# A transformer layer on one core: another hand-written order in the opening, in attention's normalisation and at the end of the output projection

## The chip, the cores and the metric

The kernel runs on one core of a Trainium2 chip as one program. The metric is the device time of one execution in microseconds. TensorE (PE in the rows) multiplies; ScalarE (ACT), VectorE (DVE) and GpSimd (POOL) work on rows of 128 partitions; SyncE (SP) issues most transfers. Each engine runs its own instruction list in order, and waits on semaphores that other engines count up.

## The reference, cut to what matters

The layer is computed for two groups of tokens, 512 of a prompt and 1024 of a sample, 1024 channels each, in fp32:

```
mod = silu(c) @ w_ada + b_ada           # shift1, scale1, gate1, shift2, scale2, gate2
h   = rmsnorm(x, g_attn) * (1 + scale1) + shift1
u, q, k, v = split(h @ w_in, 4)         # 512 columns each
q, k = rmsnorm(q, g_q), rmsnorm(k, g_k) # per head of 64
f = fourier_mix(u, w_fmix)              # real part of a 2-D DFT, then a map per group of 128
a = softmax(q k' / 8 + bias) v          # in a window of 8 rows x 16 columns of the token grid
mix = concat(rmsnorm(f), rmsnorm(a)) @ w_o
x = x + gate1 * mix
h2 = rmsnorm(x, g_ffn) * (1 + scale2) + shift2
x = x + gate2 * ((silu(h2 @ w_gate) * (h2 @ w_up)) @ w_down)
```

## The kernel before

Every fp32 product is made of three matmuls of a rounded upper half and the remaining lower half of each operand: `mm3`, lines 101 to 103. So each operand is first split: a copy that rounds (`h_hi`, `win_hi`, `wo_hi`, `wff_hi`) and a subtraction (`h_lo` and so on). The 1536 tokens are three chunks of 512 (c = 0 to 2), and 12 tiles of 128 (t). Channels are eight pieces of 128 (k). One K-step is one `mm3` on 512 tokens.

There is no planner. Each stage has a function for each engine (`run_pe`, `run_act`, ...), and the order of the calls in it is the order of the instructions on that engine.

**Opening** (`opening`). SyncE loads the first third of w_ada in eight pieces of 1 MB, x in three parts of 2 MB, and the first columns of w_in (line 282). TensorE makes the first modulation rows from the eight pieces (L674), and turns x chunk by chunk: `turn_x(n)`, n = 8c + k, four 128x128 transposes (L668) into one of two PSUM banks that change with n (`x_bank`). ScalarE modulates the turned x (`modulate`, L443). VectorE rounds it (L545) and makes the lower half for even k (L548); GpSimd makes the lower half for odd k (L349). Then TensorE runs, for each chunk, eight K-steps for u columns s = 0 and eight for s = 1. After c = 0 it turns k = 0 and 1 of c = 1. The other two thirds of w_ada come in 16 pieces through a ring of five buffers, and `rest_products` multiplies them, two at a time (`pieces_at`), between these passes. The row norms of x need squares: of each chunk's four tiles ScalarE makes two (L430) and VectorE two (L526), then ScalarE the root and VectorE the reciprocal and the scaled rows (L535). Six tiles of u columns follow (`tile(1, i)`). ScalarE evacuates each u tile (`stage_u`, L449) and GpSimd stores it to DRAM (`store`, L353).

**Attention** (`attention`): 48 steps, one for each pair of heads, column block and chunk. In step s TensorE turns the probabilities of pair s - 1 (L995), turns v tokens in two of three steps (L972), makes the scores of pair s + 1 (L986), spreads the softmax's reciprocal of pair s - 1 over 64 partitions for each head by a matmul of a broadcast column with the identity (`spread`, L1004), and multiplies probabilities by v (L1020). ScalarE makes two exponentials (L867), copies half of the turned probabilities (L875), in one of three steps v tokens (L889), and the spread scale (L881). VectorE makes the reciprocal, adds bias and takes maxima (L914), and scales the output. In the second 24 steps VectorE also does one `fold` of u each for the Fourier stage.

**Second half** (`second_half`). 48 mixing tiles: `mix_out(m)` is four K-steps of w_o columns n = m // 12 on token tile t = m % 12. VectorE gates each (L1664), GpSimd adds it to x (L1729). Row norm, turns (L1794), modulation (L1565) and split (L1681, L1684 on VectorE, L1735 on GpSimd for odd k of c = 0) give h2. Norm 0 comes before the last four mixing tiles, two turns of c = 0 after each of these, and the turns of c = 1 and c = 2 stand between the K-steps of the first gate tile on the chunk before. The feed-forward part then loops over 11 pairs of weight tiles; `pair(0)` is the first.

Other stages (q, k, v projections from 152.8 to about 360 us, Fourier from 497 to 547) lie between these.

Of the kernel before, what the change touches and what calls it, by code (L numbers as in the profile page):

```python
# [18 lines left out]
ALU = mybir.AluOpType  # L19
# [86 lines left out]
def layer(nc, x_prompt, x_sample, w_ada, b_ada, vec_rows, w_in, w_fmix, rpb_pad, masks, dft_c, dft_t1,  # L106
          dft_t0, w_o, w_gate, w_up, w_down, u_scratch, gate_rows, y_prompt, y_sample):
    ctx = ExitStack()
    with ctx:
# [42 lines left out]
        kept.u_in, kept.wf_in, kept.cs_in = [sem(f"u_in{r}") for r in range(2)], sem("wf_in"), sem("cs_in")  # L152
# [47 lines left out]
def opening(nc, at, sem, banks, kept):  # L200
# [54 lines left out]

    def x_bank(n):

        return ((2, 5), (2, 5), (0, 3))[n // KT][n % 2]
# [8 lines left out]
    def pieces_at(n):  # L267

        return {3: (0, 1), 4: (2, 3), 5: (4, 5), 6: (6, 7), 7: (8, 9), 8: (10, 11), 9: (12, 13), 10: (14, 15)}.get(n, ())

    with nc.Block() as block:
        @block.sync
        def _(sp):
# [11 lines left out]
            def load_ada(q):  # L285
                half, k = divmod(q, KT)
                if q >= 5:
                    sp.wait_ge(ada_used, q - 4)
                sp.dma_start(ada[q % 5][:], w_ada[128 * k:128 * k + 128, 4 * CH * (half + 1):4 * CH * (half + 2)]
                             ).then_inc(ada_in[q % 5], 16)  # L290
# [26 lines left out]
            load_ada(0)  # L317
            load_ada(1)
            sp.wait_ge(x_turned, 2 * KT)
            load_ada(2)  # L320
            load_ada(3)
            sp.wait_ge(x_turned, 3 * KT)
            load_ada(4)
            load_ada(5)
            load_ada(6)
# [3 lines left out]
            for q in range(7, PIECES):  # L329
                load_ada(q)  # L330
# [13 lines left out]
        def _(pool):  # L344
# [5 lines left out]

            def store(j, i, s, c):
                pool.wait_ge(bank_free, 6 * j + i + 1)
                pool.dma_start(u_scratch[(2 * j + s) * 128:(2 * j + s) * 128 + 128, CH * c:CH * c + CH],  # L353
                               u_stage[:, i % 2]).then_inc(u_stored[i % 2], 16)
# [20 lines left out]
            for c in range(NCH):  # L375
                for k in range(1, KT, 2):
                    split(KT * c + k)
                for s in range(2):
                    store(0, 2 * c + s, s, c)
            for i in range(6):  # L380
                store(1, i, *divmod(i, NCH))
                if i == 2:
                    store_gate(0)
            store_gate(1)
            rounds(pool, 0, J_QK - J_U, sq_lows)
            for s in range(2):
                pool.wait_ge(u_stored[s], 16 * 3 * J_U)
# [35 lines left out]
        def _(act):  # L423
# [22 lines left out]
            def stage_u(j, i, bank):  # L446
                act.wait_ge(z_summed, 6 * j + i + 1)
                after(act, u_stored[i % 2], 16 * (3 * j + i // 2))
                act.activation(u_stage[:, i % 2], banks[:, bank], ACT.Copy).then_inc(bank_free, 1)  # L449
# [33 lines left out]
            split_hi(act, 0, 1)  # L483
# [3 lines left out]
            square(4)  # L487
            square(5)
            root(1)
            stage_u(0, 0, 0)  # L490
            for k in range(KT):
                modulate(KT + k)
                if k in (0, 3):
                    square(8 + k // 3)
                if k == 1:
                    stage_u(0, 1, 3)
                if k == 5:
                    root(2)
            stage_u(0, 2, 1)
            for k in range(KT):  # L500
                modulate(2 * KT + k)
                if k == 3:
                    stage_u(0, 3, 4)
            split_hi(act, 1, 0)
            split_hi(act, 1, 1)
            stage_u(0, 4, 2)
            stage_u(0, 5, 5)
            for i in range(6):
                stage_u(1, i, i)
# [9 lines left out]
        def _(dve):  # L519
# [76 lines left out]
            split_lo(dve, 0, 0)  # L596
# [8 lines left out]
            split_lo(dve, 0, 1)  # L605
            for k in range(KT):
                split(k)
            square(6)
            square(7)
# [12 lines left out]
            for i in range(6):  # L622
                if i == 1:
                    rest_rows(0)
                if i == 2:
                    rest_mod(0)
                if i == 5:
# [1311 lines left out]
```

## Time and profile before

| | |
|---|---|
| runs | 1792.05, 1794.22, 1794.43 us; median 1794.22 |
| the profiled execution | 1798.47 us, its span 1796.5 us |
| TensorE busy over the span | 1741.6 us, 97% |
| VectorE, GpSimd, ScalarE busy | 804.7, 524.7, 431.3 us |
| first 44 mixing tiles and sums, 547.09 to 675.56 | TensorE busy 128.47 of 128.47 us |
| feed-forward from the third tile on, 747.30 to the end | TensorE busy 1044.70 of 1049.20 us |
| mean granted TensorE clock over the span | 0.990 |

All durations come from the one profiled execution; its own time is 4.25 us above the median of the runs. Matmuls overlap, so the spacing of starts, and not the length of one, tells what a matmul costs. A wait in square brackets behind a row is the idle time ahead of that instruction, and names what ended it. The time base is the start of the span.

### The profile page before, as it was taken

To read this page: it belongs to the slowest core of one execution; us is meant where nothing else is said; L and a number is where in the kernel's file an instruction comes from. 1 tells how busy PE (TensorE), PEld (TensorE's weight loads), DVE (VectorE), ACT (ScalarE), POOL (GpSimd) and SP (SyncE) were. 2 spreads that over 40 slices of the span, in tenths; PEclk is the share of its full clock that TensorE was granted. 3 is DMA by queue.
4 is the path that set the end of the run, shared out by engine and by line. 5 is a ranking of instruction groups with operands and counts; after the bars stand their busy time and mean duration, and the time that the engine had idled before them with its cause. 6 is when DMAs were issued, how large, how long until landed. Compare 5 with 4: busy or idle time off the path is not lost.

```text
span 1796.5 us, 22022 instructions
## 1 busy us (share of the span) xinstructions
PE 1741.6 (97%) x8437; PEld 1387.4 (77%) x8437; DVE 804.7 (45%) x1244; ACT 431.3 (24%) x779; POOL 524.7 (29%) x435
## 2 busy tenths in 40 slices
PE   5799999999999997999999999999999999999998
PEld 2557888866768885788888888888888888888887
DVE  3513886057874427352433425261524334242525
ACT  3312332177762016211111110101021111101110
POOL 0311221077736442040221405050503123050505
PEclk9999999999999998999999999999999999999999
DMA  9381014063113101001011110111010101110113
GB/s 352 141 324 39 25 34 77 12 139 78 49 36 133 55 1 47 24 24 47 24 35 35 35 35 23 35 35 35 12 47 23 47 23 35 35 35 23 35 35 140
DMA packets 98543, 108.70 MB, mean 61 GB/s; under 512 B 19655, under 2 KB 82337, under 8 KB 95161
## 3 DMA queue, kind: packets, MB, share of 16 engines
q1 hardware_dynamic: 97401, 104.82, 18.5%
q0 software_dynamic: 1088, 3.16, 0.5%
q8 instruction: 34, 0.56, 0.1%
q14 instruction: 20, 0.16, 0.0%
HBM read 98.51 MB, written 9.45 MB: 60 GB/s over the span
## 4 chain that ended last, share of the span: by engine, by line
PE 77%; DVE 2%; issue 0%; ACT 0%; POOL 0%; DVEq 0%; ACTq 0%; POOLq 0%
PE banks L101 22%; PE banks L102 22%; PE banks L103 22%; PE banks L986 2%; PE banks L995 2%; PE banks L1325 2%; PE banks L1020 2%; PE banks L1004 1%; PE banks L972 1%; DVE h_hi L1681 0%; PE banks L1794 0%; DVE xn L1674 0%; DVE h_lo L1684 0%; PE banks L1308 0%; ACT t_second L1565 0%
## 5 line engine op out<-in xcount | busy, mean ns | idle before, releaser
L1748 POOL TENSOR_TENSOR x<-x,ff_scratch 128x512 f32<-128x512 f32 x198 | 263.1, 1361 | 834.7 <-DVE ff_scratch L1641 834.1
L101 PE MATMUL banks<-h_hi,wff_hi 128*128 128x512 f32 x1056 | 414.1, 392 | 10.9 <-POOL h_lo L1735 6.1
L102 PE MATMUL banks<-h_lo,wff_hi 128*128 128x512 f32 x1056 | 412.1, 390 | 0.0
L103 PE MATMUL banks<-h_hi,wff_lo 128*128 128x512 f32 x1056 | 411.9, 390 | 0.0
L1500 DVE TENSOR_TENSOR wff_lo<-wff_raw,wff_hi 128x1024 fp32r<-128x1024 f32 x66 | 81.5, 1236 | 405.3 <-ACT wff_hi L1496 405.2
L101 PEld LDWEIGHTS banks<-h_hi,wff_hi 128*128 128x128 f32 x1056 | 199.2, 189 | 52.0 <-issue 9.3
L103 PEld LDWEIGHTS banks<-h_hi,wff_lo 128*128 128x128 f32 x1056 | 199.0, 188 | 41.5
L102 PEld LDWEIGHTS banks<-h_lo,wff_hi 128*128 128x128 f32 x1056 | 199.2, 189 | 40.3
L1641 DVE TENSOR_TENSOR ff_scratch<-banks,gate 128x512 f32<-128x512 f32 x264 | 177.3, 687 | 72.0 <-PE banks L103 49.3
L103 PE MATMUL banks<-wff_hi,ff_lo 128*128 128x512 f32 x528 | 205.4, 389 | 0.0
L102 PE MATMUL banks<-wff_lo,ff_hi 128*128 128x512 f32 x528 | 205.4, 389 | 0.0
L101 PE MATMUL banks<-wff_hi,ff_hi 128*128 128x512 f32 x528 | 205.4, 389 | 0.0
L1496 ACT ACTIVATE wff_hi<-wff_raw 128x1024 fp32r<-128x1024 f32 x66 | 70.0, 1060 | 437.5 <-DMA wff_raw<-in_w_up 354.1
L101 PE MATMUL banks<-h_hi,win_hi 128*128 128x512 f32 x384 | 153.8, 401 | 14.4 <-POOL h_lo L349 12.3
L103 PE MATMUL banks<-h_hi,win_lo 128*128 128x512 f32 x384 | 150.8, 393 | 0.0
L102 PE MATMUL banks<-h_lo,win_hi 128*128 128x512 f32 x384 | 150.6, 392 | 0.0
L101 PEld LDWEIGHTS banks<-wff_hi,ff_hi 128*128 128x128 f32 x528 | 99.2, 188 | 20.6
L103 PEld LDWEIGHTS banks<-wff_hi,ff_lo 128*128 128x128 f32 x528 | 99.1, 188 | 20.5
L102 PEld LDWEIGHTS banks<-wff_lo,ff_hi 128*128 128x128 f32 x528 | 99.1, 188 | 20.5
L1628 DVE TENSOR_TENSOR ff_raw<-banks,ff_scratch 128x512 f32<-128x512 f32 x66 | 45.5, 689 | 138.0 <-PE banks L103 138.0
L101 PEld LDWEIGHTS banks<-h_hi,win_hi 128*128 128x128 f32 x384 | 72.5, 189 | 38.9 <-POOL h_lo L349 15.1
L1526 ACT ACTIVATE ff_hi<-ff_raw 128x512 fp32r<-128x512 f32 x66 | 41.7, 632 | 243.5 <-DVE ff_raw L1628 243.5
(169 smaller groups left out, 2106.0 us busy)
## 6 DMA issues: line engine op xcount, KB each, us to landing
ada_rest<-in_w_ada SPq DMA_DIRECT2D x16, 1024.0 KB, 8.6
wff_raw<-in_w_gate SPq DMA_DIRECT2D x22, 512.0 KB, 4.7
wff_raw<-in_w_up SPq DMA_DIRECT2D x22, 512.0 KB, 3.9
wff_raw<-in_w_down SPq DMA_DIRECT2D x22, 512.0 KB, 3.2
ada<-in_w_ada SPq DMA_DIRECT2D x8, 1024.0 KB, 13.8
win_raw<-in_w_in SPq DMA_DIRECT2D x16, 512.0 KB, 3.9
x_first<-in_x_sample SPq DMA_DIRECT2D x2, 2048.0 KB, 16.5
wo_raw<-in_w_o SPq DMA_DIRECT2D x4, 1024.0 KB, 5.0
```

The costliest lines, as they stand in the source:

```text
L101: pe.matmul(out, lhs[0], rhs[0], start=start, stop=False)
L102: pe.matmul(out, lhs[0], rhs[1], start=False, stop=False)
L103: return pe.matmul(out, lhs[1], rhs[0], start=False, stop=stop)
L986: pe.matmul(banks[:, hh, 0:n], queries, keys, start=True, stop=True).then_inc(qk_done, 1)
L995: last = pe.transpose(banks[:, 2 + hh, 128 * j:128 * j + 128], s_ring[:, w % 2, hh, 128 * j:128 * j + 128], ident[:])
L1020: last = pe.matmul(banks[64 * hh:64 * hh + 64, 4 + w % 2, 0:128], v_tok[:, b * NVT + V_TILE0[c] + j, 64 * hh:64 * hh + 64], pt_ring[:, w % ...
L1496: act.activation(w_hi[:, i % 3], w_raw[:, i % 3], ACT.Copy).then_inc(w_split_hi, 1)
L1500: dve.tensor_tensor(w_lo[:, i % 3], w_raw[:, i % 3], w_hi[:, i % 3].bitcast(F32), ALU.subtract).then_inc(w_ready, 1)
L1526: act.activation(ff_hi[:, f, CH * c:CH * c + CH], ff_raw[:, f, CH * c:CH * c + CH], ACT.Copy).then_inc(ff_hi_s, 1)
L1628: dve.tensor_tensor(part, banks[:, 3 + c], scratch[:, c], ALU.mult).then_inc(product, 1)
L1641: dve.tensor_tensor(scratch[:, n % 3], banks[:, (6 + n) % 8], gate2[:, REQ[t // 4], 512 * half:512 * half + 512], ALU.mult).then_inc(d_gat ...
L1748: pool.tensor_tensor(part, part, scratch[:, n % 3], ALU.add).then_inc(d_added, 1)
```

## The change

In the opening all eight pieces of the first w_ada load stand ahead of w_in in SyncE's queue, and two of the later pieces are loaded without a wait. `x_bank` uses three banks, so that `turn_x(n)` waits for the modulation of n - 3 and not n - 2. Five turns of c = 1 stand in the second pass of c = 0, the other three in the first pass of c = 1, and all eight of c = 2 in the second pass of c = 1. The later pieces of w_ada come one place earlier, and the modulation turn stands before the six tiles. Squares of c = 1 stand among the modulations (ScalarE) and splits (VectorE) of c = 0. ScalarE issues the stores of u.

In attention ScalarE first copies the two reciprocals of a pair of heads to 64 columns each (`widen`, a 128x128 array), and TensorE transposes that array at the head of the next step. The output scaling comes one step later. The folds start at step 12 and take 36 steps.

In the second half the mixing tiles of n = 2 and 3 go chunk by chunk (`SEQ`). The turns of c = 0 stand behind mixing tiles 34 to 37, those of c = 1 behind 42 to 45, and those of c = 2 within the second and third first-pair tiles. The row norm is two rows on VectorE and two on ScalarE instead of three and one, and all odd lower halves are GpSimd's.

```diff
@@ opening
+    SLOT = (0, 1, 0, 1, 2, 3, 0, 1, 2, 3, 4, 0, 1, 2, 3, 4)
...
-        return ((2, 5), (2, 5), (0, 3))[n // KT][n % 2]
+        return ((2, 5, 7), (2, 5, 7), (0, 3, 7))[n // KT][n % KT % 3]
...
-        return {3: (0, 1), 4: (2, 3), 5: (4, 5), 6: (6, 7), 7: (8, 9), 8: (10, 11), 9: (12, 13), 10: (14, 15)}.get(n, ())
+        return (2 * n - 2, 2 * n - 1) if 1 <= n <= 8 else ()
...
-            for k in range(3, 6):
+            for k in range(3, KT):
                 load_ada0(k)
             load(0, 0)
-            load_ada0(6)
-            load_ada0(7)
             load(0, 1)
             load_x(1)
             load_x(2)
+            load_ada(0)
+            load_ada(1)
...
+                act.wait_ge(bank_free, 6 * j + i + 1)
+                act.dma_start(u_scratch[(2 * j + s) * 128:(2 * j + s) * 128 + 128, CH * c:CH * c + CH],
+                              u_stage[:, i % 2]).then_inc(u_stored[i % 2], 16)
...
             for k in range(KT):
                 split(k)
-            square(6)
-            square(7)
+                if k in (3, 5):
+                    square(6 + k // 5)
+                if k == 4:
+                    split_lo(dve, 0, 1)
...
-                if n >= 2:
-                    pe.wait_ge(t_ready, n - 1)
+                if n >= 3:
+                    pe.wait_ge(t_ready, n - 2)
...
-                    if c == 1 and k == 3:
-                        turn_x(2 * KT)
-                        turn_x(2 * KT + 1)
+                    if c == 0 and k >= 3:
+                        turn_x(KT + k - 3)
+                    if c == 1:
+                        turn_x(2 * KT + k)
@@ attention
+    FOLD_STEPS = list(range(PAIRS_A // 4, PAIRS_A // 2)) + list(range(PAIRS_A // 2, PAIRS_A, 2))
...
+        def widen(w):
+            act.wait_ge(recip_done, w + 1)
+            if w >= 2:
+                act.wait_ge(scale_spread, w - 1)
+            act.activation(recips[:, w % 2].rearrange("p (h f) -> p h f", h=2),
+                           bass.AP(stats, 4 * PAIRS_A + 2 * w, [[6 * PAIRS_A, 128], [1, 2], [0, HEAD]]), ACT.Copy
+                           ).then_inc(widened, 1)
...
-            if s:
-                copy_scale(s - 1)
+            if s >= 2:
+                copy_scale(s - 2)
+            if 1 <= s <= PAIRS_A:
+                widen(s - 1)
...
-            for hh in range(2):
-                last = pe.matmul(banks[64 * hh:64 * hh + 64, 6, 0:128],
-                                 stats[:, 2, 2 * w + hh:2 * w + hh + 1].broadcast_to((128, 64)), ident[:],
-                                 start=True, stop=True)
-            last.then_inc(scale_spread, 1)
+            pe.transpose(banks[:, 6, 0:128], recips[:, w % 2], ident[:]).then_inc(scale_spread, 1)
@@ second_half
+    SEQ = [(n, t) for n in range(2) for t in range(TT)] + [
+        (n, t) for c in range(NCH) for n in range(2, OS) for t in range(4 * c, 4 * c + 4)]
+    FIRST = [SEQ.index((n, 0)) for n in range(OS)]
+    TURN = [34, 42]
...
+        square(8)
+        square(9)
+        square(10)
+        split_hi(act, 0, 1)
+        square(11)
+        root(2)
+        norm(2)
+        silu(act, 0, 0)
...
+            ff_tile(0, 0)
+            h_ready(1)
+            pe.wait_ge(gated, TT * OS - 2)
+            for k in range(KT):
+                ff_step(0, 1, k)
+                if k >= 2:
+                    turn(2 * KT + k - 2)
+            pe.wait_ge(w_ready, 2)
...
+            mix_out(m)
+            for c, first in enumerate(TURN):
+                if first <= m < first + 4:
+                    turn(KT * c + 2 * (m - first))
+                    turn(KT * c + 2 * (m - first) + 1)
```

The first place is TensorE's list in the opening where c = 0's second pass ends and c = 1's first begins, of before (`x_first` is x, `ident` the identity of a transpose):

```order
L101 MATMUL banks<-h_hi,win_hi 128x512
L102 MATMUL banks<-h_lo,win_hi 128x512
L103 MATMUL banks<-h_hi,win_lo 128x512
L668 MATMUL banks<-ident,x_first 128x128 x12
L101 MATMUL banks<-h_hi,win_hi 128x512
L102 MATMUL banks<-h_lo,win_hi 128x512
L103 MATMUL banks<-h_hi,win_lo 128x512
L668 MATMUL banks<-ident,x_first 128x128 x4
L101 MATMUL banks<-h_hi,win_hi 128x512
L102 MATMUL banks<-h_lo,win_hi 128x512
L103 MATMUL banks<-h_hi,win_lo 128x512
```

and of the kernel after, where L659 is the same transpose and L665 the product of the later w_ada pieces:

```order
L659 MATMUL banks<-ident,x_first 128x128 x4
L101 MATMUL banks<-h_hi,win_hi 128x512
L102 MATMUL banks<-h_lo,win_hi 128x512
L103 MATMUL banks<-h_hi,win_lo 128x512
L659 MATMUL banks<-ident,x_first 128x128 x4
L665 MATMUL banks<-ada_rest_73,silu_c 2x512 x4
L665 MATMUL banks<-ada_rest_74,silu_c 2x512 x4
L101 MATMUL banks<-h_hi,win_hi 128x512
L102 MATMUL banks<-h_lo,win_hi 128x512
L103 MATMUL banks<-h_hi,win_lo 128x512
L659 MATMUL banks<-ident,x_first 128x128 x4
L101 MATMUL banks<-h_hi,win_hi 128x512
```

The twelve transposes that stood in one block between the passes (with the next four behind the first K-step) have moved, four at a time, between the K-steps of the second pass; a pair of w_ada pieces stands in the gap.

The second place is TensorE's list in three steps of attention, of before (`s_ring` holds probabilities, `v_pair` values, `stats` the reciprocals):

```order
L1004 MATMUL banks<-ident,stats 64x128 x2
L1020 MATMUL banks<-pt_ring,v_tok 64x128 x6
L995 MATMUL banks<-ident,s_ring 128x128 x4
L972 MATMUL banks<-ident,v_pair 128x128 x4
L986 MATMUL banks<-z 128x384 x2
L1004 MATMUL banks<-ident,stats 64x128 x2
L1020 MATMUL banks<-pt_ring,v_tok 64x128 x4
L995 MATMUL banks<-ident,s_ring 128x128 x6
L972 MATMUL banks<-ident,v_pair 128x128 x2
L986 MATMUL banks<-z 128x256 x2
L1004 MATMUL banks<-ident,stats 64x128 x2
L1020 MATMUL banks<-pt_ring,v_tok 64x128 x6
```

and of after (L1006 is the new transpose, of `recips`):

```order
L1006 MATMUL banks<-ident,recips 128x128
L998 MATMUL banks<-ident,s_ring 128x128 x4
L975 MATMUL banks<-ident,v_pair 128x128 x4
L989 MATMUL banks<-z 128x384 x2
L1019 MATMUL banks<-pt_ring,v_tok 64x128 x4
L1006 MATMUL banks<-ident,recips 128x128
L998 MATMUL banks<-ident,s_ring 128x128 x6
L975 MATMUL banks<-ident,v_pair 128x128 x2
L989 MATMUL banks<-z 128x256 x2
L1019 MATMUL banks<-pt_ring,v_tok 64x128 x6
L1006 MATMUL banks<-ident,recips 128x128
```

Two matmuls between the scores and the values of a step have become one at the step's head, ahead of the turn of the probabilities. On ScalarE the same three steps stood so before:

```order
L867 ACTIVATE s_ring,stats<-s_ring,stats 128x384
L875 ACTIVATE pt_ring<-banks 128x256
L867 ACTIVATE s_ring,stats<-s_ring,stats 128x384
L889 ACTIVATE v_tok<-banks 128x512
L881 ACTIVATE scale_sb<-banks 128x128
L867 ACTIVATE s_ring,stats<-s_ring,stats 128x384
L875 ACTIVATE pt_ring<-banks 128x384
L867 ACTIVATE s_ring,stats<-s_ring,stats 128x384
L881 ACTIVATE scale_sb<-banks 128x128
```

and stand so after (L874 copies the spread scale, L881 widens the reciprocals):

```order
L860 ACTIVATE s_ring,stats<-s_ring,stats 128x384
L868 ACTIVATE pt_ring<-banks 128x256
L860 ACTIVATE s_ring,stats<-s_ring,stats 128x384
L890 ACTIVATE v_tok<-banks 128x512
L874 ACTIVATE scale_sb<-banks 128x128
L881 ACTIVATE recips<-stats 128x128
L860 ACTIVATE s_ring,stats<-s_ring,stats 128x384
L868 ACTIVATE pt_ring<-banks 128x384
L860 ACTIVATE s_ring,stats<-s_ring,stats 128x384
L874 ACTIVATE scale_sb<-banks 128x128
L881 ACTIVATE recips<-stats 128x128
```

In each step the widening has come in behind the copy of the scale, and in the step with `v_tok` both stand behind that copy.

The third place is TensorE's list in the mixing, where the first turns of c = 0 stand; of before, behind mixing tile 44:

```order
L102 MATMUL banks<-wo_lo_2399,h_hi 128x512
L103 MATMUL banks<-wo_hi_2398,h_lo 128x512
L1794 MATMUL banks<-ident,xn 128x128 x8
L101 MATMUL banks<-wo_hi_2398,h_hi 128x512
L102 MATMUL banks<-wo_lo_2399,h_hi 128x512
```

and of after, behind mixing tile 34 (L1790 is the turn, `xn_early` the two halves of the normed rows):

```order
L102 MATMUL banks<-wo_lo_2363,h_hi 128x512
L103 MATMUL banks<-wo_hi_2362,h_lo 128x512
L1790 MATMUL banks<-ident,xn_early_2404 128x128 x2
L1790 MATMUL banks<-ident,xn_early_2405 128x128 x2
L1790 MATMUL banks<-ident,xn_early_2404 128x128 x2
L1790 MATMUL banks<-ident,xn_early_2405 128x128 x2
L101 MATMUL banks<-wo_hi_2362,h_hi 128x512
L102 MATMUL banks<-wo_lo_2363,h_hi 128x512
L103 MATMUL banks<-wo_hi_2362,h_lo 128x512
```

The turns have moved ten tiles up, in front of other mixing tiles, and read the rows from two arrays.

## Rows read from the trace of the kernel before

**Rows 1.** Busy time by stretch (start:end, length, engines, clock, DMA): opening, attention, mixing's end.

```profile
36.65:152.83 116.18, 101.34 (x512) 68.17 (x513) 42.28 (x64) 32.54 (x49) 26.79 (x25) 0.96 0.54 206
361.00:497.00 136.00, 134.50 (x1265) 93.04 (x1264) 99.73 (x378) 100.46 (x307) 101.50 (x112) 0.97 0.40 88
...
675.56:747.30 71.74, 58.30 (x277) 47.35 (x277) 43.69 (x67) 35.38 (x50) 11.31 (x8) 0.90 0.11 37
```

**Rows 2.** TensorE's timeline in the opening: start, length, line, idle before and its releaser.

```profile
38.13 0.47 PE L101 MATMUL banks<-h_hi,win_hi 128*128 128x512 f32 x1 [0.82 <-DVE h_lo L548]
...
49.66 0.50 PE L101 MATMUL banks<-h_hi,win_hi 128*128 128x512 f32 x1 [1.63 <-POOL h_lo L349]
...
50.46 0.40 PE L101 MATMUL banks<-h_hi,win_hi 128*128 128x512 f32 x1
...
51.83 0.39 PE L101 MATMUL banks<-h_hi,win_hi 128*128 128x512 f32 x1
...
78.99 1.90 PE L674 MATMUL banks<-ada_rest,silu_c 128*2 128x512 f32 x16
80.82 0.66 PE L668 MATMUL banks<-ident,x_first 128*128 128x128 f32 x4
```

**Rows 3.** TensorE's timeline, the two last pieces of the first w_ada load.

```profile
28.34 1.89 PE L674 MATMUL banks<-ada,silu_c 128*2 128x512 f32 x8 [2.33 <-DMA ada<-in_w_ada]
30.93 1.89 PE L674 MATMUL banks<-ada,silu_c 128*2 128x512 f32 x8 [0.70 <-DMA ada<-in_w_ada]
```

**Rows 4.** GpSimd's (POOL) and then VectorE's (DVE) timeline beside each other in the opening.

```profile
44.72 1.28 POOL L349 TENSOR_TENSOR h_lo<-t_first,h_hi 128x512 fp32r<-128x512 f32 x1 [1.89 <-DVE h_hi L545]
47.42 2.18 POOL L349 TENSOR_TENSOR h_lo<-t_first,h_hi 128x512 fp32r<-128x512 f32 x1 [1.43 <-DVE h_hi L545]
...
47.26 1.22 DVE L526 CUSTOM_DVE_ANT_0 dump_dve<-x_first 128x1024 f32<-128x1024 f32 x1
...
48.63 2.05 DVE L526 CUSTOM_DVE_ANT_0 dump_dve<-x_first 128x1024 f32<-128x1024 f32 x1
```

**Rows 5.** Attention: TensorE's timeline of one step and a head, then ScalarE's (ACT).

```profile
374.68 0.44 PE L1004 MATMUL banks<-ident,stats 128*64 128x128 f32 x4
374.95 0.83 PE L1020 MATMUL banks<-pt_ring,v_tok 128*64 128x128 f32 x12
375.71 0.66 PE L995 MATMUL banks<-ident,s_ring 128*128 128x128 f32 x4
376.20 0.60 PE L972 MATMUL banks<-ident,v_pair 128*128 128x128 f32 x4
...
378.38 0.88 PE L995 MATMUL banks<-ident,s_ring 128*128 128x128 f32 x6
...
375.17 0.28 ACT L881 ACTIVATE scale_sb<-banks 128x128 f32<-128x128 f32 x1 [0.58 <-PE banks L1004]
...
377.06 0.58 ACT L889 ACTIVATE v_tok<-banks 128x512 f32<-128x512 f32 x1
```

**Rows 6.** TensorE's timeline, the first feed-forward K-step after the last mixing tile.

```profile
695.15 0.77 PE L101 MATMUL banks<-h_hi,wff_hi 128*128 128x512 f32 x1 [6.11 <-POOL h_lo L1735]
```

**Rows 7.** SyncE's issues: a backlogged pair, then all of line 289, shortest/median/longest.

```profile
5.71 15.02 SPq L275 DMA_DIRECT2D ada<-in_w_ada  x2
...
L289 SPq DMA_DIRECT2D ada_rest<-in_w_ada x16: 327/430/1207, 46.8 to 130.6; - x16
...
DMA to landing us min/median/max: 4.9/8.6/13.5
```

**Rows 8.** The page's costliest groups, and its DMA issues with their time to landing.

```profile
L1500 DVE TENSOR_TENSOR wff_lo<-wff_raw,wff_hi 128x1024 fp32r<-128x1024 f32 x66 | 81.5, 1236 | 405.3 <-ACT wff_hi L1496 405.2
...
L1496 ACT ACTIVATE wff_hi<-wff_raw 128x1024 fp32r<-128x1024 f32 x66 | 70.0, 1060 | 437.5 <-DMA wff_raw<-in_w_up 354.1
...
wff_raw<-in_w_up SPq DMA_DIRECT2D x22, 512.0 KB, 3.9
...
wo_raw<-in_w_o SPq DMA_DIRECT2D x4, 1024.0 KB, 5.0
```

More of the change, by code:

```diff
@@ L1026, in run_pe @@
         turn_v(0, 1)
-        for s in range(PAIRS_A + 1):
-            if s:
+        for s in range(PAIRS_A + 2):
+            if s >= 2:
+                spread(s - 2)
+            if 1 <= s <= PAIRS_A:
                 turn(s - 1)
@@ L1699, in run_dve @@
                 mix_recip(1)
-            if m % TT == 1 and m > TT and m // TT + 1 < OS:
-                split_o(m // TT + 1)
-        norm(0)
-        for i in range(4):
-            gate_mix(TT * OS - 4 + i)
-            if i == 2:
-                split_lo(dve, 0, 0)
-            split(2 * i)
-            split(2 * i + 1)
-        norm(1)
-        for k in range(KT):
-            split(KT + k)
+            if m in (FIRST[1] + 1, FIRST[2] + 1):
+                split_o(2 + (m > FIRST[2]))
+            if m == FIRST[3]:
+                split_lo(dve, 0, 0)
+            for c, first in enumerate(TURN):
+                if m == first - 1:
+                    norm(c)
+                if first <= m < first + 4:
+                    split(KT * c + 2 * (m - first))
+                    split(KT * c + 2 * (m - first) + 1)
         norm(2)
@@ L1821, in run_pe, with ff_tile, h_ready, first_tiles @@
-        waits_split(pe, KT * NCH - 1)
+                last.then_inc((g_summed, u_summed)[kind], 1)
+        def ff_tile(i, c):
+            for k in range(KT):
+                ff_step(i, c, k)
+        def h_ready(c):
+            waits_split(pe, KT * c + KT - 2)
+            waits_split(pe, KT * c + KT - 1)
+        def first_tiles():
+            pe.wait_ge(w_ready, 1)
+            h_ready(0)
+            pe.wait_ge(gated, TT * OS - 3)
+            ff_tile(0, 0)
+            h_ready(1)
+            pe.wait_ge(gated, TT * OS - 2)
+            for k in range(KT):
+                ff_step(0, 1, k)
+                if k >= 2:
+                    turn(2 * KT + k - 2)
+            pe.wait_ge(w_ready, 2)
+            pe.wait_ge(gated, TT * OS)
+            for k in range(KT):
+                ff_step(1, 0, k)
+                if k < 2:
+                    turn(3 * KT - 2 + k)
+            h_ready(2)
+            ff_tile(0, 2)
+            pe.wait_ge(t_ready, NCH * KT)
+            ff_tile(1, 1)
+            ff_tile(1, 2)
@@ L1860, in pair @@
                 last.then_inc(d_summed, 1)
+        for m in range(TT * OS):
+            if m == 2 * TT - 6:
+                f_sums()
+            mix_out(m)
+            for c, first in enumerate(TURN):
+                if first <= m < first + 4:
+                    turn(KT * c + 2 * (m - first))
+                    turn(KT * c + 2 * (m - first) + 1)
         pair(0)
```

290 lines of the change are left out of this document (121 added, 169 removed).

## The prediction

> **What bounds the kernel now.** I read the share of busy time by stage first, then TensorE's own timeline in the stages that the change touches. In [rows 1] TensorE is busy 134.50 of 136.00 us in attention, and the stage table ahead shows the same of the feed-forward loop and of the first 44 output-projection tiles: work alone sets these. Two stretches differ. The opening up to 152.83 has 101.34 busy of 116.18, and the stretch from the last mixing tiles to the third feed-forward tile pair has 58.30 of 71.74, at a granted clock of 0.90. Nothing outside TensorE is full anywhere: ScalarE, the nearest, is at 100.46 of 136.00 in attention. So a microsecond is won where TensorE waits or runs below full clock, or where one of its matmuls goes.
>
> **Opening.** A K-step is three matmuls. At full clock [rows 2] show one starting at 50.46 and the second after it at 51.83: 0.685 each, 0.228 a matmul. A pair of pieces of the rest of w_ada takes 80.82 - 78.99 = 1.83, a turn of four transposes about 0.40. From the first K-step at 38.13 to 152.83 are 114.7 us. In them stand 48 K-steps of u (32.7), 21 turns (8.4), 8 pairs (14.6), 6 tiles of 8 K-steps (32.8) and some 1.4 of modulation rows: 89.9. The other 24.8 are lost to waits and to half clock. [Rows 2] show one place, 1.63 before 49.66 on GpSimd's lower half of h, and c=1 has more of them; between c=0 and c=1 turn, modulation and split run one after the other with TensorE waiting for each.
>
> The change alters each. (a) All eight pieces of the first w_ada load come ahead of w_in. In [rows 3] the piece behind w_in is waited for 2.33, the next one 0.70; the difference, 1.6 to 1.7, goes, and the first K-step comes at 36.4. The lower half of the first w_in part stays one VectorE instruction ahead of the splits, so it costs nothing new. (b) With three banks and five turns of c=1 inside the second pass of c=0, c=1 finds its first five operands ready. By hand: c=0's first pass ends at 47.7 instead of 50.46, its second with five turns at 55.3, the first pair at 57.2, c=1's passes at 65 and 76 with a pair after each (66.8, 77.8), c=2's at 83.3 and 90.6 with pairs (85.1, 92.4). Then six tiles and three pairs, 38.3 with the modulation turn, end near 131.3, and the wait for coef brings 132.3. (c) Some 6 us of waits stay in this sum: c=0's K-steps 5 and 7 on GpSimd, and the norm rows before c=2's first turn. So 152.83 becomes 132 to 133, a gain of 20; with a microsecond off for contention I take 19. If everything that I leave as waiting goes, 22 is the limit I allow. If the squares put among the splits cost GpSimd what they cost it in [rows 4], eight times 0.9, it is 12.
>
> The transfers are no new bound by this order: the two pieces loaded without waiting come behind x, and the four that follow are asked for 8 to 10 us before use, against 8.6 in the median to landing [rows 7]. Should each pair be late by 1 us, seven pairs cost 7, inside the 12.
>
> **Attention.** Per step two 64-row matmuls go and one transpose comes. In [rows 5] the old pair takes 374.95 - 374.68 = 0.27, and four transposes take 376.20 - 375.71 = 0.49, so 0.12 each: 48 x 0.15 = 7.2. What may take it back is ScalarE. It gets 48 widening instructions; its nearest row, the 128x128 copy of the spread scale, is 0.28 [rows 5], so 13.4 us come on top of 100.46 in a stretch of 129: 88%, below TensorE's 97%. The wait is local: the transpose now heads TensorE's step, so that a late widening holds up everything behind it there, the turn of the probabilities first, and with it the copies on ScalarE and VectorE. In two steps of three the second exponential ends a microsecond before TensorE's next step, and the scale copy and the widening need 0.5. In the third step the copy of v tokens stands before them: 377.06 + 0.58 + 0.5 = 378.14 against a head at 378.38, which the shortening itself pulls forward by up to 0.45 in three steps. So 0 to 0.35 may be lost there in each of 16, 0 to 5.6 in all. I take 2.2 lost: gain 5, with -2 to 7 as bounds (below zero if the extra step at the end, about 1.5, and the folds on VectorE beside it also cost). Folds over 36 steps instead of 24 lie on VectorE, 99.73 busy of 136.00, which does not set the step; u has been loaded well before step 12.
>
> **Mixing and first feed-forward tiles.** From 547.09 to 747.30 are 200.2. TensorE's longest wait there is the 6.11 before 695.15 for the split [rows 6]; the 0.77 of the K-step at 695.15 beside 0.48 in [rows 2] after short ones shows the lower clock that follows it. Work in this stretch is 128.5, four tiles of 12 matmuls (10.9), 24 turns and six tiles of 8 K-steps (42), so 18.8 are lost. The change puts the turns of c=0 and c=1 inside the mixing, where other tiles cover norm, modulation and split. After it stand 128.5 for 44 mixing tiles, 10.9 for the last four, 16 turns (6.4) and two waits of 0.45 for the norm before tiles 34 and 42: 146.6. Behind: six tiles of 5.46 and eight turns (3.2), 36.0, and waits. The part that is late next is c=2. ScalarE splits the up-projection weights ahead of the last square: asked for 0.4 after the last mixing tile's end, landed 3.9 later, split in 1.06 [rows 8], then a square of about 1.2, root and reciprocal 0.5 and the norm's two rows on each engine, about 2.2, end 9.2 after that tile. TensorE wants the turn after a tile and three K-steps, at 7.5: 1.75 lost, and I add 0.6 behind the table load of silu. Sum 146.6 + 38.3 = 184.9, gain 15.3; I take 14.4, since short waits can still cost some half clock, as those at 695 did.
> The fourth output weights must now be split for tile 28 and not 36. They are asked for after tile 23 and land 5.0 later; by twice the splits of half the size, 2 x 1.06 on ScalarE and 2 x 1.24 on VectorE [rows 8], they are ready 10 us after tile 23, of the 10.9 that four tiles take. Each microsecond beyond is lost one for one. Bounds: 18 if no wait at c=2 stays, 10 if the norms and weights are each 1.5 us later.
>
> **Sum.** 19 + 5 + 14.4 = 38.4. Against its own profiled execution, 1798.5 - 38.4 = 1760. That execution lies 4.25 above the median of the runs, 1794.2, so I predict 1756.
>
> **Rivals.** (1) The widening eats attention's gain: ScalarE ends each third step 0.35 late. For it: the margin of 0.24. Against it: ScalarE no longer idles for the spread, 0.58 at 375.17. Time 1761.
> (2) VectorE's squares and GpSimd's splits collide, and c=2's norm and the fourth weights come late: 12 to 15 in the opening, 10 to 12 in the tail, so 25 to 29 with attention between 2 and 3: 1765 to 1770. In [rows 4] a split on GpSimd is 1.28 alone and 2.18 when a square on VectorE has begun 0.16 before it; the next square, begun while that split runs, is 2.05 instead of 1.22. So each square now put among the splits may hold GpSimd up by 0.9. The Trainium skill, "SBUF — State Buffer", section "Who interferes with whom", says that two such instructions contend for one port pair, held as an exclusive lock by whichever starts first. The trace agrees: the 0.90 is about the rest of the square, and the 0.83 of the next square about the rest of the split. Against this rival: in before the squares already stood among c=1's splits, and the added slack in banks hides part.
> (3) Slower: the u stores, now issued by ScalarE, block it. SyncE's two issues took 15.02 behind a backlog [rows 7], 7.5 each. Six stores lie among the modulations that TensorE waits for; above 6.4 each they cost 6 x 6.4 = 38.4 and the whole gain is gone; at 7.5 the time is 1801. Against it: the later pieces cost SyncE 0.43 in the median, 1.2 at most [rows 7], at a DMA share of 0.54 [rows 1], and the backlog of the first 20 us has gone by the first store at 49. The Trainium skill, "DMA: Bandwidth & Descriptors", section "Queues, rings and completion order", says that SyncE and ScalarE each own a row of rings on the same 16 engines. By it SyncE's backlog would not stop ScalarE's issue, and the stores would cost what the short issues do, 12 x 0.43 beside other work; no run here shows ScalarE issuing under load.
> (4) The change does not do what it says, and TensorE waits as before: 1794. The instruction order speaks against it, since the turns do stand elsewhere.
>
> **How the numbers follow.** My forecast 0.55 (gain 33 to 43: 1751 to 1761), rival 1 alone 0.12, rival 2 0.25, rival 3 0.03, rival 4 0.02, better than all 0.03. The parts' bounds add to 47 and to 20, so 1747 to 1774 holds the forecast with rivals 1 and 2. About 0.2%, 3.6 us, is what a measurement of this kernel can tell from no change: faster 0.95, same 0.02, slower 0.03.
>
> **What would show it.** First K-step near 36.4, none of the waits of 1.6 on GpSimd at c=1, the q, k, v stage starting near 132; attention's steps 0.1 shorter than 2.68; no wait above 2 us between the last mixing tile and the feed-forward loop, and its start some 39 earlier. I am wrong if TensorE waits for the widening in every step, for a ScalarE that issues stores, or for pieces of w_ada.

## The result and the profile after

The changed kernel takes 1761.48 us (median of 4 runs, 1760.1 to 1763.42), before 1794.26 (4 runs): a ratio of 0.9821, interval 0.9804 to 0.9838, 32.8 us less. 1756 was predicted, 1747 to 1774 the range. The profiled execution of after took 1760.1, its span 1758.3, so it lies 1.4 below its median, where that of before lies 4.2 above.

Busy time by stretch in after, as in [rows 1] (start:end, length, then PE, PEld, DVE, ACT, POOL, TensorE's granted clock, DMA share and GB/s): opening from the first K-step, attention, all mixing tiles, the first six feed-forward tiles.

```profile
34.26:137.58 103.32, 95.87 (x504) 65.05 (x505) 44.37 (x62) 31.55 (x49) 21.38 (x16) 0.98 0.63 242
345.53:477.38 131.85, 127.42 (x1121) 86.89 (x1121) 99.57 (x379) 106.58 (x354) 101.62 (x112) 1.00 0.42 90
...
527.48:670.02 142.54, 141.11 (x666) 117.38 (x666) 75.88 (x92) 38.27 (x52) 82.77 (x57) 1.00 0.14 51
670.02:709.00 38.98, 36.95 (x177) 29.67 (x176) 16.84 (x23) 17.89 (x24) 6.81 (x6) 1.00 0.21 68
```

The opening's 114.70 has become 103.32, attention's 136.07 (from its first score on) 131.85. The wait of 6.11 at the end of the mixing [rows 6] is gone: TensorE is busy 141.11 of 142.54. The granted clock is 1.00 in three of the four, where [rows 1] had 0.97 in attention and 0.90 at the mixing's end.

TensorE in the opening of after (start, length, wait in brackets), to set against [rows 2]:

```profile
34.26 0.47 PE L101 MATMUL banks<-h_hi,win_hi 128*128 128x512 f32 x1 [0.90 <-DVE h_lo L542]
...
44.46 0.50 PE L101 MATMUL banks<-h_hi,win_hi 128*128 128x512 f32 x1 [2.76 <-POOL h_lo L353]
...
45.47 0.80 PE L101 MATMUL banks<-h_hi,win_hi 128*128 128x512 f32 x1
...
47.16 0.80 PE L101 MATMUL banks<-h_hi,win_hi 128*128 128x512 f32 x1
...
79.91 0.66 PE L659 MATMUL banks<-ident,x_first 128*128 128x128 f32 x4 [1.93 <-ACT t_first L435]
...
137.58 0.50 PE L101 MATMUL banks<-h_hi,win_hi 128*128 128x512 f32 x1 [0.48 <-DVE coef L624]
```

The first K-step is at 34.26, the q, k, v stage at 137.58. The turns of c = 1 no longer show a wait, but c=0's sixth K-step waits 2.76, then the next two stand 1.69 apart (47.16 - 45.47) instead of 0.68: the granted clock is 0.50 from 45.3 to 48.6, and 0.2 of the 1.69 is a further wait. c=2's eighth turn waits 1.93 at 79.91. What lies behind these stands on the other engines. VectorE:

```profile
37.55 2.05 DVE L520 CUSTOM_DVE_ANT_0 dump_dve<-x_first 128x1024 f32<-128x1024 f32 x1 [0.39 <-DMA x_first<-in_x_sample]
...
40.60 1.22 DVE L394 TENSOR_TENSOR win_lo<-win_raw,win_hi 128x1024 fp32r<-128x1024 f32 x1
41.73 0.42 DVE L539 CAST h_hi<-t_first 128x512 fp32r<-128x512 f32 x1
42.07 1.22 DVE L520 CUSTOM_DVE_ANT_0 dump_dve<-x_first 128x1024 f32<-128x1024 f32 x1
```

GpSimd:

```profile
42.23 2.17 POOL L353 TENSOR_TENSOR h_lo<-t_first,h_hi 128x512 fp32r<-128x512 f32 x1 [3.71 <-DVE h_hi L539]
```

ScalarE, with all its u stores in the last row (shortest, median and longest ns):

```profile
37.55 1.06 ACT L422 ACTIVATE dump_act<-x_first 128x1024 f32<-128x1024 f32 x1 [1.95 <-DMA x_first<-in_x_sample]
...
78.02 0.60 ACT L441 ACTIVATE u_stage<-banks 128x512 f32<-128x512 f32 x1 [3.29 <-PE banks L103]
...
79.08 2.79 ACT L435 ACTIVATE t_first<-banks,mod,coef 128x512 f32<-128x512 f32 x4 [0.46 <-ACT u_stage L441]
...
L443 ACTq DMA_DIRECT2D u_scratch<-u_stage x12: 326/326/349, 53.3 to 137.4; - x12
```

VectorE's square at 37.55 and ScalarE's both begin when x's second load lands, after a wait of 1.95 on ScalarE in front of c=0's fifth modulation. That square and the lower half of w_in's second part (40.60) stand before VectorE rounds k = 5 at 41.73, and the second square starts at 42.07, 0.16 before GpSimd's split of k = 5, which then takes 2.17, as in [rows 4]. At 78.02 ScalarE has waited 3.29 for c=1's second pass to end, and c=2's modulations 4 to 7 stand behind it (79.08). The stores cost 0.33 each.

TensorE in attention: the head, in before, of the step three behind the one at 374.68 in [rows 5],

```profile
382.72 0.44 PE L1004 MATMUL banks<-ident,stats 128*64 128x128 f32 x4
```

and, of after, one step with v tokens' last two turns and then one with a wait:

```profile
375.71 0.33 PE L1006 MATMUL banks<-ident,recips 128*128 128x128 f32 x1
375.87 0.82 PE L998 MATMUL banks<-ident,s_ring 128*128 128x128 f32 x6
...
377.47 0.88 PE L1019 MATMUL banks<-pt_ring,v_tok 128*64 128x128 f32 x12
378.28 0.33 PE L1006 MATMUL banks<-ident,recips 128*128 128x128 f32 x1
...
380.90 0.88 PE L1019 MATMUL banks<-pt_ring,v_tok 128*64 128x128 f32 x12 [0.79 <-issue]
```

A step is 378.28 - 375.71 = 2.57; three of before take 382.72 - 374.68 = 8.04, 2.68 each. The one transpose takes 375.87 - 375.71 = 0.16. At 380.90 the values wait 0.79. VectorE just before:

```profile
378.86 0.33 DVE L1132 COPY uo<-u 128x2 f32<-128x2 f32 x2
379.11 1.22 DVE L1135 TENSOR_TENSOR uo<-u 128x255 f32<-128x255 f32 x1
380.25 0.54 DVE L929 COPY pt_ring<-banks 128x384 f32<-128x384 f32 x1
```

The fold at 379.11 takes 1.22 beside GpSimd and stands ahead of the copy of the probabilities at 380.25, for which the values wait: the profile names no releaser there, and the experiment fold_pt below shows it.

TensorE's waits for the row norms of c = 0, 1 and 2 in after, where [rows 6] had 6.11 for the split:

```profile
626.43 1.09 PE L1790 MATMUL banks<-ident,xn_early 128*128 128x128 f32 x8 [0.71 <-DVE xn_early L1670]
...
652.74 1.09 PE L1790 MATMUL banks<-ident,xn_early 128*128 128x128 f32 x8 [0.72 <-DVE xn_early L1670]
...
679.08 0.63 PE L1790 MATMUL banks<-ident,xn 128*128 128x128 f32 x4 [1.42 <-DVE xn L1670]
```

### The profile page after: what moved, and what is told of

It is laid out like the page before. It is cut to its first block, busy times and chain, and to the rows that moved or that the text cites. A ratio compares the mean times of both kernels' runs of the same rounds, so it can differ in the third digit from the quotient of the medians.

```text
span 1758.3 us, 21827 instructions
## 1 busy us (share of the span) xinstructions
PE 1718.3 (98%) x8293; PEld 1370.7 (78%) x8293; DVE 803.3 (46%) x1235; ACT 440.5 (25%) x830; POOL 528.6 (30%) x431
## 4 chain that ended last, share of the span: by engine, by line
PE 78%; issue 1%; DVE 1%; ACT 0%; DMA 0%; POOL 0%; DVEq 0%; ACTq 0%; POOLq 0%
PE banks L101 23%; PE banks L102 23%; PE banks L103 23%; PE banks L989 2%; PE banks L1019 2%; PE banks L1325 2%; PE banks L998 2%; PE banks L1006 1%; PE banks L975 1%; PE banks L1790 1%; PE banks L1308 0%; DMA wff_raw<-in_w_up 0%; DVE alt L1231 0%; PE banks L1753 0%; PE banks L1336 0%
```

## The experiments

Each time is a median of 5 to 12 runs against before on the same chip, except where said. First the parts one by one: `opening`, `attention` with the fold schedule, and `second_half` of after, each put alone into before.

```diff
# op_only, at_only, sh_only
-    opening | attention, fold | second_half   of before
+    opening | attention, fold | second_half   of after
```

> The kernel before with the opening of the changed kernel alone. Theory A (the three parts add, and the profile's stage differences are what each is worth): the q, k, v stage starts 15 us earlier, the time is about 15 us below before (0.9915). Rival B (the parts help each other, since shorter waits keep the clock up in later stages): under 12 us alone. In its profile the stretch from the first mixing tile on is as in before.

> The kernel before with attention and the fold schedule of the changed kernel alone. Theory A: undisturbed steps 2.57 us instead of 2.68, some stalls of 0.26 beside folds, so 2 to 4 us below before (0.998 to 0.999), the attention stretch 1.6 to 4.2 shorter, the larger number only where before began it at half clock. Rival B: the widening holds TensorE in every third step and nothing is gained, within 1 us of before.

> The kernel before with the second half of the changed kernel alone. Theory A: 13 to 16 us below before (0.991 to 0.993) in the timed runs; in the profiles the stretch from the first mixing tile to the third feed-forward tile is 181 to 183 us, and that of before is 200 only with the half-clock stretches of its profiled run and about 197 without. Rival B: the gain needs the other parts, under 10 us alone.

| kernel | median us | ratio to before | interval | less than before (1794.38) |
|---|---|---|---|---|
| op_only | 1779.45 | 0.9915 | 0.990 to 0.993 | 14.9 |
| at_only | 1790.31 | 0.9977 | 0.9966 to 0.9988 | 4.1 |
| sh_only | 1779.57 | 0.9914 | 0.9899 to 0.9929 | 14.8 |

Together 33.8, and the whole is 32.8: within the intervals the parts add, and none needs another, as theory A said. What it said of the stretches in the profiles held less well. From the first mixing tile to the third feed-forward tile, sh_only takes 185.1 and not 181 to 183, and op_only takes 197.5 where the first profile of before had 200.3. These profiles also show what the same code does from run to run. Starts and stretches read from each TensorE timeline, with the granted clock in attention:

| profile (mean clock) | first K-step | q, k, v stage from | opening stretch | attention stretch | clock there |
|---|---|---|---|---|---|
| before (0.990) | 38.13 | 152.83 | 114.70 | 136.07 | 0.97 |
| at_only (0.991): opening of before, attention of after | 36.94 | 149.43 | 112.49 | 134.50 | 0.97 |
| sh_only (0.995): opening and attention of before | 37.90 | 150.13 | 112.23 | 135.21 | 0.99 |
| op_only (0.989): opening of after, attention of before | 35.71 | 138.68 | 102.97 | 133.79 | 1.00 |
| after (0.999) | 34.26 | 137.58 | 103.32 | 131.85 | 1.00 |
| after again (0.994) | 36.10 | 139.12 | 103.02 | 131.86 | 1.00 |

The first profile of before had the longest opening of three with the same code, by 2.2 and 2.5 us, and the longest attention of three, by 0.9 and 2.3. Like with like, attention of after is shorter by 1.6 at a clock of 0.97 (at_only beside before) and by 1.9 at 1.00 (after beside op_only); the 4.1 of at_only's runs, with 2.2 to 6.1 as its interval, is more than these traces show, and the difference is open. The unaltered kernel once more:

> The changed kernel again, unaltered, on the same chip as the next. Theory A (its first profile, at a clock of 0.999, and the profile of before, at 0.990, lie at opposite ends of what each does, so the profiles differ by 38 where the runs differ by 33): median 1760 to 1763, 0.981 to 0.983 of before. Rival B (the 38 of the profiles is what the change is worth): 0.978 to 0.980.

It took 1762.08 (1761.58 to 1763.87), 0.9821 of before, interval 0.9807 to 0.9835. Theory A on the size: the 38.2 between the two profiled spans is 5 to 6 more than the change is worth. Its reason is not borne out as put: over 17 timed runs of before the fastest, 1790.01, had a mean clock of 0.988 and the slowest, 1799.25, 0.987, so the mean clock does not tell a long run from a short one. By stretches the profile of before was longer than its siblings by 2.2 to 2.5 in the opening, 0.9 to 2.3 in attention, and 1.6 to 3.2 from the first mixing tile to the first feed-forward tile (148.06; op_only 146.44, at_only 144.85). Within a stretch the clock does tell: from the first mixing tile to the third feed-forward tile it is 0.949 in before, 0.957 in op_only and 0.965 in at_only, and the same code takes 200.3, 197.5 and 196.4; attention is in the table.

Next attention: the fold behind the copy that the values wait for, and the folds back on steps 24 to 47.

```diff
# fold_pt
-            if s in FOLD_STEPS:
-                mix.fold(dve, FOLD_STEPS.index(s))
             if 1 <= s <= PAIRS_A:
                 copy_pt(s - 1)
+            if s in FOLD_STEPS:
+                mix.fold(dve, FOLD_STEPS.index(s))
# fold24
-    FOLD_STEPS = list(range(PAIRS_A // 4, PAIRS_A // 2)) + list(range(PAIRS_A // 2, PAIRS_A, 2))
+    FOLD_STEPS = list(range(PAIRS_A // 2, PAIRS_A))
```

> The changed kernel with each fold of u one place later on VectorE, behind the copy of the probabilities instead of ahead of it. Theory A (attention falls short of 48 x 0.15 because a fold ahead of that copy delays TensorE's values): the steps of 2.83 and 3.42 us in attention become 2.57 to 2.65, attention 2 to 3.5 us shorter, time 2 to 3 us below the changed kernel. Rival B (the stalls come from GpSimd's masks and VectorE's load, not from the order): no change within 1 us, stalls elsewhere in the step.

> The changed kernel with the folds of u on steps 24 to 47, one a step, as in before. Theory A (a stall belongs to a fold in a heavy step, not to how many steps they are spread over): within 1 us of the changed kernel, the stalls of 0.26 in the second half of attention instead of the first. Rival B (spreading over 36 steps is what makes room): 2 to 4 us slower than the changed kernel.

VectorE of fold_pt in the step that waited 0.79:

```profile
380.18 0.56 DVE L929 COPY pt_ring<-banks 128x384 f32<-128x384 f32 x1 [0.35 <-PE banks L998]
380.65 0.38 DVE L1132 COPY uo<-u 128x2 f32<-128x2 f32 x2
380.94 0.41 DVE L1135 TENSOR_TENSOR uo<-u 128x255 f32<-128x255 f32 x1
```

and its TensorE:

```profile
380.07 0.92 PE L989 MATMUL banks<-z 64*128 64x384 f32 x4
380.92 0.88 PE L1019 MATMUL banks<-pt_ring,v_tok 128*64 128x128 f32 x12
```

The copy comes 0.35 after VectorE is free, the fold behind it, and the values follow the scores at once, 0.85 later. Attention takes 129.40 instead of 131.85; of the steps ahead of the one with the Fourier maps, those of 2.82 or more fall from ten (3.43 and 3.18 among them) to three of 2.83 to 2.89. In these three TensorE waits for the widened reciprocals, 0.19 to 0.26 each:

```profile
392.36 0.33 PE L1006 MATMUL banks<-ident,recips 128*128 128x128 f32 x1 [0.25 <-ACT recips L881]
```

That is theory A on place and size in the profile; in the runs it is 1760.36 (1760.01 to 1762.7), 1.1 below after, short of its 2 to 3 and less than the ranges of the two tell apart. fold24 took 1763.1 (1760.57 to 1763.82), 0.9829 of before (0.9816 to 0.9843). Its stalls sit in the second half, as theory A had it (3.43 and 3.17 once, 2.82 to 2.83 seven times). Its attention is 134.32, and the 2.5 more than in after are the start: the second step's transpose comes 9.68 after the first score, in after 7.06. The start ran at half clock (0.97 over the stretch). At that clock the same attention with the folds over 36 steps takes 134.50 in at_only, 134.2 in sq_act and 134.4 in stage_late, so like with like the spreading makes no difference in the traces. The 1.6 in the runs lies between the theories.

Then the opening, the part that fell short.

```diff
# sq_act
-        return t % 4 >= 2 and t >= 4          # on_dve(t)
+        return t % 4 >= 2 and t >= 8
...
                 if k in (3, 5):
                     square(4 + k // 5)
+            square(6)
+            square(7)
             root(1)
# stage_late
-                if k in (0, 4):
-                    stage_u(0, 2 + k // 4, k // 4, 1)
+                if k == 0:
+                    stage_u(0, 2, 0, 1)
                 modulate(2 * KT + k)
+            stage_u(0, 3, 1, 1)
```

> The changed kernel with c=1's two VectorE squares moved from among c=0's splits to ScalarE, behind c=0's last modulation. Theory A (in the opening the square holds up GpSimd's split of k=5, TensorE waits 2.76 us and then runs at half clock for four K-steps): the split takes 1.28 instead of 2.17, the wait is under 1 us, no half clock behind it, the q, k, v stage starts 3 to 5 us earlier and the time is 3 to 5 below the changed kernel. Rival B (the norm of c=1 comes later on ScalarE and the first turn of c=1 waits instead): a new wait of 2 us or more before that turn, less than 1 us gained.

> The changed kernel with ScalarE's evacuation of the u tile of c=1, s=1 behind c=2's last modulation instead of behind its fourth. Theory A (ScalarE stands at that evacuation until c=1's pass ends, so that TensorE waits 1.93 us for c=2's eighth turn): that wait goes, 1.5 to 2 us gained. Rival B (the wait only moves to c=2's first K-steps or to the bank that the evacuation frees): under 0.5 us gained.

GpSimd of sq_act at the same K-step, c=0's sixth:

```profile
42.27 1.38 POOL L353 TENSOR_TENSOR h_lo<-t_first,h_hi 128x512 fp32r<-128x512 f32 x1 [2.56 <-DVE h_hi L541]
```

and its TensorE, from c=0's first K-step on:

```profile
35.44 0.47 PE L101 MATMUL banks<-h_hi,win_hi 128*128 128x512 f32 x1 [0.82 <-DVE h_lo L544]
...
43.71 0.50 PE L101 MATMUL banks<-h_hi,win_hi 128*128 128x512 f32 x1 [1.84 <-POOL h_lo L353]
...
45.95 0.50 PE L101 MATMUL banks<-h_hi,win_hi 128*128 128x512 f32 x1 [0.59 <-POOL h_lo L353]
...
46.75 0.40 PE L101 MATMUL banks<-h_hi,win_hi 128*128 128x512 f32 x1
```

The split is 1.38 instead of 2.17, the wait 1.84 instead of 2.76, and the K-steps behind it are at full clock (0.80 from 45.95 to 46.75). c=0's first pass, eight K-steps, takes 46.75 - 35.44 = 11.31, in after 14.35. The opening stretch is 100.27 (135.71 - 35.44), 2.7 to 3.1 shorter than in the two profiles of after, and no wait before c=1's first turn has come. The mechanism is theory A's; the wait that stays is larger than it said, the stage starts 1.9 to 3.4 earlier and not 3 to 5, and in the runs the kernel took 1761.03 (1758.8 to 1763.54), which tells no gain apart. In stage_late the turn goes without a wait into the pair:

```profile
79.80 0.60 PE L660 MATMUL banks<-ident,x_first 128*128 128x128 f32 x4
80.33 1.90 PE L666 MATMUL banks<-ada_rest,silu_c 128*2 128x512 f32 x16
```

1.93 are gone there; the opening stretch is 101.29, at a start at half clock. The runs took 1760.37 (1758.89 to 1762.47): theory A in the trace, unclear in the time. The three edits together, and then with c=1's squares later:

```diff
# all3 = fold_pt + sq_act + stage_late; all3b = all3 and
-                if k in (3, 5):
-                    square(4 + k // 5)
-            square(6)
-            square(7)
+                if k in (5, 6, 7):
+                    square(k - 1)
             root(1)
...                                    # VectorE, behind c=0's splits
+            square(7)
```

> The changed kernel with three edits together: folds behind the copy of the probabilities, c=1's squares on ScalarE, the evacuation behind c=2's last modulation. If each is worth what theory A says of it alone, 6 to 9 us below the changed kernel, 1753 to 1756. If the opening's edits only move waits, as the rivals say, 1 to 2 us, near 1760.

> The three edits together, with c=1's squares later still: three on ScalarE behind c=0's sixth to eighth modulation, one on VectorE behind c=0's last split. Theory A (ScalarE's first square stands in front of c=0's fifth modulation and waits there for x's second load, which costs c=0's K-steps 4 to 7 up to 2 us): the waits of 2 us before K-step 5 go, at most 1 us before the first turn of c=1 comes in, 0.5 to 2 us below the three edits alone, 1756 to 1758. Rival B (the norm of c=1 is then the late one): a wait of 1.5 us or more before the first turn of c=1 and no gain, 1758 to 1760.

all3 took 1758.35 (1755.96 to 1759.42), 0.9805 of before (0.9792 to 0.9818): 3 below the changed kernel, short of 6 to 9. Its opening has the squares of sq_act, but its sixth K-step waits 1.97 and half clock follows again:

```profile
43.59 0.50 PE L101 MATMUL banks<-h_hi,win_hi 128*128 128x512 f32 x1 [1.97 <-POOL h_lo L353]
...
45.83 0.79 PE L101 MATMUL banks<-h_hi,win_hi 128*128 128x512 f32 x1
```

So the full clock in sq_act is one profile's, and not shown to come from the edit. The profiles also show where much of what the edits won went. Attention, 129.40 in fold_pt at a clock of 1.00, takes 131.88 in all3, which ran at 0.50 from 344.9 to 351.6. The stretch from the first mixing tile to the third feed-forward tile takes 183.3 in all3 and 183.5 in fold_pt, with 0.50 behind the first tiles, against 181.7 in after at 1.00. In sq_act and stage_late attention began at half clock as well (134.2 and 134.4 long), which hides 2.3 to 2.5 of what their openings gained. Why these places ran at half clock in one profile and not in another is open, and of the timed runs only the mean clock is known, so for the medians this is not shown.

all3b took 1757.67 (1756.61 to 1758.11), 0.9793 of before, interval 0.9779 to 0.9807, beside 1762.08 (1761.58 to 1763.87) of the changed kernel on the same chip: a version that beats both. Between it and all3 the runs decide nothing. TensorE in it, the last row the first turn of c=1:

```profile
42.61 0.50 PE L101 MATMUL banks<-h_hi,win_hi 128*128 128x512 f32 x1 [1.38 <-POOL h_lo L353]
...
45.75 0.50 PE L101 MATMUL banks<-h_hi,win_hi 128*128 128x512 f32 x1 [1.49 <-POOL h_lo L353]
...
49.28 0.60 PE L659 MATMUL banks<-ident,x_first 128*128 128x128 f32 x4
```

K-step 5 waits 1.38, K-step 7 1.49, and the first turn of c=1 not at all; the opening stretch is 98.63 instead of 103. Theory A is right that ScalarE's early square cost something at K-step 5 (1.38 instead of 1.84 in sq_act), wrong that the wait would go. c=0's first pass as a whole did not get shorter: 11.85 (46.55 - 34.70), in sq_act 11.31, both at full clock. VectorE's one square, now behind c=0's last split, starts 0.16 before GpSimd's split of k = 7 and holds it up as the other did that of k = 5:

```profile
43.36 1.21 DVE L521 CUSTOM_DVE_ANT_0 dump_dve<-x_first 128x1024 f32<-128x1024 f32 x1
...
43.52 2.18 POOL L353 TENSOR_TENSOR h_lo<-t_first,h_hi 128x512 fp32r<-128x512 f32 x1 [0.96 <-DVE h_hi L540]
```

All four squares of c=1 on ScalarE, as late as here, were not tried. What still stands on VectorE ahead of k = 5 is the lower half of w_in's second part (1.22 at 40.60 in after); moving it was not tried either.

## Why the prediction was right, and where it was not

The number was 5.5 low, inside its range, and the largest of its steps was off by 4.

**From the profile to the runs.** The sum against before's own execution, 1760, is what the profiled execution of after then took, 1760.1. That is luck twice over. I took off 4.25 for before's profile lying above its median, as if after's would too; it lay 1.4 below. And the parts missed on both sides.

**Opening, 19 forecast, 14.9 measured (op_only).** This is the step that failed. The order of the first loads gave at least what I said (first K-step 34.3 to 36.1, forecast 36.4), and the early turns took the handover's waits away. But I kept 6 us of waits, and 13 were lost to waits and half clock (103.3 less the 89.9 of work): c=0's first pass takes 14.35 from its first K-step where I had 11.3, c=1's first pass 9.0 for 7.8, its second 11.4 for 9.2. Two causes are measured in the traces. One is VectorE's squares among c=0's splits: without them (sq_act) the split of k = 5 is 0.8 shorter, the wait 0.9, and the pass takes the 11.3 that I had; how much of the 3.0 saved was half clock behind that wait is not shown apart. The other is the u evacuation in ScalarE's list ahead of c=2's fifth modulation (stage_late: 1.93). Of the 7.4 by which the stretch exceeds my 95.9, all3b's trace takes back 4.7; the cause of the rest stays open, and no single edit to the opening is told apart in the runs. The evacuation I had not priced at all: I counted the stores that moved to ScalarE, not what stands behind the evacuation they hang on.

**Attention, 5 forecast, 4.1 measured with 2.2 to 6.1 as its interval (at_only).** The size lies in the interval, the reason does not hold. The transpose at the step's head costs 0.16 and not 0.12, so 2.57 instead of 2.68 a step, 5 in 48. The widening, for which I took off 2.2, did not hold TensorE: it put ScalarE at 106.58 of 131.85, 6 more than before and not 13.4; of TensorE's waits in after none is for it, and only when the folds had moved (fold_pt) did three of 0.19 to 0.26 come. What took 2 to 3 back was a term that I had put at nothing in the sum and named for its lower bound alone, the folds: ahead of the copy of the probabilities they make TensorE wait ten times in after, 2.8 in all, and in before, whose step was longer, once, 0.3 at the first fold; fold_pt gives 2.45 back in the trace. So the nearness of 5 and 4.1 is in part luck: my 5 was 7.2 less 2.2 for a widening that cost nothing in after, and like with like the traces show only 1.6 to 1.9.

**Mixing, 14.4 forecast, 14.8 measured (sh_only).** The waits came as worked out: 0.71 and 0.72 for the norms (0.45 each forecast), 1.42 at c=2 (1.75). The fourth weights were in time. Two errors of mine hid in the row of 128.47 for "44 tiles": 45 tiles lie in it (540 matmuls of 12 a tile), and its granted clock is 0.97, where the same code ran at 0.99 and 1.00 in op_only and at_only. So the stretch to the last mixing tile came out at 142.5, not 146.6, and the two profiles differ by 18.6 up to the third feed-forward tile; the runs show 14.8. The mechanism is the forecast's, but that the number came so close owes something to luck: the after side was put too long by these two errors, and the before side was one long profile's.

**Rivals.** Rival 1's time, 1761, is the measured one, but not by its mechanism. Rival 2 is partly what happened in the opening: VectorE's square holds up GpSimd's split. By "SBUF — State Buffer" of the Trainium skill, "Who interferes with whom", a VectorE instruction with two inputs in SBUF, as the square is, contends with a GpSimd instruction that reads SBUF, and the one that starts first keeps the shared ports. The traces agree: 2.17 with the square at 42.07, 1.38 without it in sq_act, 2.18 with the square at 43.36 in all3b. In the tail it did not come. Rival 3 is dead: ScalarE's 12 stores take 0.33 each in the median and 0.35 at most, against the 6.4 from which it decides.

## What to carry to other kernels

Sum the terms from rows, but don't carry one profile's distance from the median over to the changed kernel: compare stretches of identical code in two or three profiles before a difference of 2 or 3 us in one stretch is put down to an edit. When an engine's list is reordered, price what stands behind every instruction in it that waits (here an evacuation that waits for a pass), and look which instruction of another engine it will run beside (here a square beside a split): not only at the instruction that was moved. When a step gets shorter, look again at the side work that fitted into it; moving it behind the copy that the bound engine waits for gave 2.45 back in the trace here.

## What was not expected of the hardware

One stretch of the same code differs by 2 us from profile to profile: the q, k, v stretch is 207.94 to 208.00 in all twelve, but the opening of before ranged over 112.2 to 114.7, its attention over 133.8 to 136.1, with a granted clock there of 0.97 in the longest and 1.00 in the shortest. In before, mixing began at half clock behind 24 small matmuls (0.63 each for the next ones); in after the same place ran at 0.39.

```profile
547.59 0.63 PE L102 MATMUL banks<-wo_lo,h_hi 128*128 128x512 f32 x1
...
527.80 0.39 PE L102 MATMUL banks<-wo_lo,h_hi 128*128 128x512 f32 x1
```

What decides between the two is open. Waits of 2.6 to 2.8 before c=0's sixth K-step were followed by K-steps at half clock in five profiles of after's order there; so were 2.31 in stage_late, which has the same order for c=0, and 1.97 in all3. Behind 1.84 in sq_act, and behind 1.38 and 1.49 in all3b, the K-steps were at full clock.
